# Split memory products: raw weights through four buffers, the second layer's normed memory earlier in a tile, and another order at the tail

## What is computed

```python
# first block, feed-forward: D = 1024, D_FF = 2816
ff = silu(h2 @ w_ffn_gate) * (h2 @ w_ffn_up)
x  = x + ff @ w_ffn_down
# second block, layer 0: conformer convolution, 31 taps
u = h @ w_pw1 + b_pw1;  a, gate = split(u);  u = a * sigmoid(gate)
u = depthwise_conv(u, 31 taps) + b_dw
u = silu(layernorm(u)) @ w_pw2 + b_pw2
# both layers l = 0, 1 of the second block: keys and values of the memory (256 rows)
mem_n = rmsnorm(mem, norm_memsrc_g[l])
k = mem_n @ mem_wk[l];  v = mem_n @ mem_wv[l]
```

## Time and profile before

| What | Value |
| --- | --- |
| Median of three runs | 2304.02 us (2301.10 to 2304.34) |
| The profiled execution's own time | 2304.21 us |
| Its span | 2302.0 us |
| PE busy | 2230.8 us (97%) |
| DVE, ACT, POOL busy | 1336.5, 979.6, 398.1 us |
| Mean granted PE clock, as a share of full | 0.988 |

### The profile page before, as it was taken

How to read it: one execution, slowest core, us unless ns; L and a number is a source line. 1 busy time by engine, 2 the same in 40 slices (tenths; PEclk the granted TensorE clock), 3 DMA queues, 4 the chain that set the end, 5 groups by cost and what they waited for, 6 DMA issues and landing times.

```text
span 2302.0 us, 31272 instructions
## 1 busy us (share of the span) xinstructions
PE 2230.8 (97%) x10680; PEld 1809.6 (79%) x10680; DVE 1336.5 (58%) x1904; ACT 979.6 (43%) x1486; POOL 398.1 (17%) x338
## 2 busy tenths in 40 slices
PE   8999999999999987889999999999999999999998
PEld 6787788877787776768888888887777888888887
DVE  5567756555554756876465445476565646454545
ACT  6775644433343555564333222245445333222222
POOL 2232002111010445644030000030000404000003
PEclk9999999999999988999999999999999999999999
DMA  4222223468686454461123333332221222333332
GB/s 146 64 65 70 68 83 100 137 170 254 170 236 191 130 192 142 155 206 55 56 83 92 96 98 100 91 93 79 65 65 56 83 65 74 102 98 93 100 92 91
DMA packets 413080, 253.36 MB, mean 110 GB/s; under 512 B 14832, under 2 KB 394224, under 8 KB 412976
## 3 DMA queue, kind: packets, MB, share of 16 engines
q1 hardware_dynamic: 412080, 249.68, 36.5%
q0 software_dynamic: 896, 2.33, 0.3%
HBM read 232.56 MB, written 18.87 MB: 109 GB/s over the span
## 4 chain that ended last, share of the span: by engine, by line
PE 73%; DMA 6%; DVE 5%; issue 4%; POOLq 4%; ACT 3%; SPq 2%; DVEq 1%; POOL 1%; ACTq 0%
PE bank L1944 20%; PE bank L1946 20%; PE bank L1945 20%; POOLq L667 4%; DMA m_raw<-in_w_ffn_up 4%; DMA m_raw<-in_w_ffn_down 2%; PE bank L1924 2%; DVE m_w_lo L1255 2%; PE bank L2417 1%; PE bank L2394 1%; PE bank L2097 1%; SPq L399 1%; PE bank L2523 1%; PE bank L2490 1%; ACT m_w_hi L692 1%
## 5 line engine op out<-in xcount | busy, mean ns | idle before, releaser
L692 ACT ACTIVATE m_w_hi<-m_raw 128x1024 fp32r<-128x1024 f32 x332 | 351.4, 1058 | 718.6 <-PE bank L1946 685.2
L1944 PE MATMUL bank<-m_h_hi,m_w_hi 128*128 128x512 f32 x1504 | 608.6, 405 | 12.5 <-DVE m_w_lo L1255 11.4
L1946 PE MATMUL bank<-m_h_hi,m_w_lo 128*128 128x512 f32 x1504 | 587.0, 390 | 0.0
L1945 PE MATMUL bank<-m_h_lo,m_w_hi 128*128 128x512 f32 x1504 | 586.5, 390 | 0.0
L1255 DVE TENSOR_TENSOR m_w_lo<-m_raw,m_w_hi 128x1024 fp32r<-128x1024 f32 x332 | 444.0, 1337 | 122.4 <-ACT m_w_hi L692 116.9
L1944 PEld LDWEIGHTS bank<-m_h_hi,m_w_hi 128*128 128x128 f32 x1504 | 282.9, 188 | 89.2 <-DVE m_w_lo L1255 19.1
L1946 PEld LDWEIGHTS bank<-m_h_hi,m_w_lo 128*128 128x128 f32 x1504 | 282.4, 188 | 60.3
L1945 PEld LDWEIGHTS bank<-m_h_lo,m_w_hi 128*128 128x128 f32 x1504 | 283.2, 188 | 54.9 <-issue 2.2
L1944 PE MATMUL bank<-m_f_hi,m_w_hi 128*128 128x512 f32 x688 | 269.2, 391 | 1.9 <-DVE m_w_lo L1255 1.7
L1946 PE MATMUL bank<-m_f_hi,m_w_lo 128*128 128x512 f32 x688 | 267.8, 389 | 0.0
L1945 PE MATMUL bank<-m_f_lo,m_w_hi 128*128 128x512 f32 x688 | 267.8, 389 | 0.0
(11 more groups left out here) (399 smaller groups left out, 3286.8 us busy)
## 6 DMA issues: line engine op xcount, KB each, us to landing
m_raw<-in_ff_w SPq DMA_DIRECT2D x256, 256.0 KB, 3.0
mem_low<-m_mem_raw_lo SPq DMA_DIRECT2D x32, 512.0 KB, 3.2
m_mem_w_low<-mem_low SPq DMA_DIRECT2D x32, 512.0 KB, 7.0
m_raw<-in_conv_pw_w SPq DMA_DIRECT2D x48, 256.0 KB, 3.1
m_raw<-in_w_in SPq DMA_DIRECT2D x47, 256.0 KB, 3.3
m_raw<-in_w_ffn_gate SPq DMA_DIRECT2D x44, 256.0 KB, 5.5
m_raw<-in_w_ffn_up SPq DMA_DIRECT2D x44, 256.0 KB, 5.3
m_raw<-in_w_ffn_down SPq DMA_DIRECT2D x40, 256.0 KB, 5.6
```

Source lines behind the costliest of these rows:

```text
L692: act.activation(WH[:, v % 2], RAW[:, v % 2], ACT.Copy).then_inc(s.w_hi, 1)
L1944: pe.matmul(o, high[:, r, k, :], hi, start=start, stop=False)
L1945: pe.matmul(o, high[:, r, k, :], lo, start=False, stop=False)
L1946: last = pe.matmul(o, low[:, r, k, :], hi, start=False, stop=stop)
```

## The change

Three parts. (1) In the FFN the raw memory weights go through four buffers at other addresses, are loaded ahead of unit n + 1 instead of n + 3, and wait for the store four memory units earlier. (2) In tiles 1 to 4 of the convolution `memory_high` stands ahead of ACT's first `mem_high` of the tile and `memory_low` ahead of the evacuation of unit A; in all tiles from 1 on, ACT forms products 6 to 8 ahead of the tile's further roundings, and 9 to 12 after them. (3) At the tail, ACT rounds memory units 25 and 26 ahead of tile 7's first products and evacuates unit 28 after the squares; PE forms the last mean ahead of memory unit 28.

```diff
-        SW = [at(f"mem_raw{i}", 144 + 4 * i, [P, D]) for i in range(3)]
-        SWL = [at(f"mem_raw_lo{i}", 144 + 4 * i, [P, D], F32R) for i in range(3)]
-        SWH = [at(f"mem_raw_hi{i}", 156 + 4 * i, [P, D], F32R) for i in range(2)]
+        SW = [at(f"mem_raw{i}", kb, [P, D]) for i, kb in enumerate((120, 124, 160, 194))]
+        SWL = [at(f"mem_raw_lo{i}", kb, [P, D], F32R) for i, kb in enumerate((120, 124, 160, 194))]
+        SWH = [at(f"mem_raw_hi{i}", kb, [P, D], F32R) for i, kb in enumerate((148, 152))]
...
+            def stored(i):
+                sp.wait_ge(sw_io[i % 4], 32 * (i // 4 + 1))
+
             def split_in(i):
-                if i >= 3:
-                    sp.wait_ge(sw_io[i % 3], 32 * (i // 3))
-                mem_raw(i, SW[i % 3], sw_io[i % 3])
+                if i >= 4:
+                    stored(i - 4)
+                mem_raw(i, SW[i % 4], sw_io[i % 4])
...
             for i, n in enumerate(MEM_SPLIT_AT):
                 split_at.setdefault(ffn + n + 5, []).append(lambda i=i: split_out(i))
             for i, n in enumerate(MEM_SPLIT_AT):
-                split_at.setdefault(ffn + n + 3, []).append(lambda i=i: split_in(i))
+                split_at.setdefault(ffn + n + 1, []).append(lambda i=i: split_in(i))
...
+                if 1 <= m <= 4:
+                    for k in range(2 * m - 2, 2 * m):
+                        memory_high(k, 1)
                 mem_high(first)
                 step(None)
+                if m > 0:
+                    products(m - 1, SUM_TAPS // 2, SUM_TAPS - 4)
                 for i in range(first + 1, min(last, first + 3)):
                     mem_high(i)
                 mem_out(first)
                 if m > 0:
-                    products(m - 1, SUM_TAPS // 2, SUM_TAPS)
-                if 1 <= m <= 4:
-                    for k in range(2 * m - 2, 2 * m):
-                        memory_high(k, 1)
+                    products(m - 1, SUM_TAPS - 4, SUM_TAPS)
                 step(None)
...
-            products(KD - 1, 0, 4, *last)
             mem_high(25)
             mem_high(26)
+            products(KD - 1, 0, 4, *last)
             mem_out(24)
...
             mem_out(27)
-            mem_out(28)
             for i in range(29, MEM_UNITS):
                 mem_high(i)
...
                 act.activation((LG, CA)[k % 2][:], CV[:, k, :], ACT.Square).then_inc(s.ln_sq, 1)
+            mem_out(28)
             norm(eps=EPSL, src=OB)
...
-                step(scaled(CA[:]), [chunk(0)])
-                if 1 <= m <= 4:
-                    for k in range(2 * m - 2, 2 * m):
-                        memory_low(k, 1)
+                def memory_lows():
+                    if 1 <= m <= 4:
+                        for k in range(2 * m - 2, 2 * m):
+                            memory_low(k, 1)
+
+                step(scaled(CA[:]), [chunk(0), memory_lows])
                 step(scaled(CG[:], None, s.cv_g), [chunk(1)])
...
-            for i in range(MEM_TAIL + 2, MEM_TAIL + 4):
-                mem_product(i)
+            mem_product(MEM_TAIL + 2)
             conv_mean(KD - 1).then_inc(s.ln_mean, 1)
+            mem_product(MEM_TAIL + 3)
```

More of the change, by code:

```diff
@@ L375, in build @@
         mw_in = [s.mw_in0, s.mw_in1, s.mw_in2, s.mw_in3, s.mw_in4]
-        sw_io = [s.sw_io0, s.sw_io1, s.sw_io2]
+        sw_io = [s.sw_io0, s.sw_io1, s.sw_io2, s.sw_io3]
         mem_low = nc.dram_tensor("mem_low", (MEM_UNITS, P, D), F32, kind="Internal").ap()
@@ L477, in mem_raw @@
                 sp.dma_start(dst[:].rearrange("p (a b) -> p a b", a=w.shape[1]), w).then_inc(done, 16)
+            def stored(i):
+                sp.wait_ge(sw_io[i % 4], 32 * (i // 4 + 1))
             def split_in(i):
-                if i >= 3:
-                    sp.wait_ge(sw_io[i % 3], 32 * (i // 3))
-                mem_raw(i, SW[i % 3], sw_io[i % 3])
+                if i >= 4:
+                    stored(i - 4)
+                mem_raw(i, SW[i % 4], sw_io[i % 4])
             def split_out(i):
                 sp.wait_ge(s.sw_lo, i + 1)
-                sp.dma_start(mem_low[i], SWL[i % 3][:].bitcast(F32)).then_inc(sw_io[i % 3], 16)
+                sp.dma_start(mem_low[i], SWL[i % 4][:].bitcast(F32)).then_inc(sw_io[i % 4], 16)
             ffn = U.n
@@ L492, in _ @@
             for i, n in enumerate(MEM_SPLIT_AT):
-                split_at.setdefault(ffn + n + 3, []).append(lambda i=i: split_in(i))
+                split_at.setdefault(ffn + n + 1, []).append(lambda i=i: split_in(i))
             def splits():
-                if U.n == ffn + MEM_SPLIT_AT[0] + 3:
+                if U.n == ffn + MEM_SPLIT_AT[0] + 1:
                     sp.wait_ge(s.unit_done, ffn)
@@ L517, in _ @@
                     assert not split_at
-                    for i in range(3):
-                        sp.wait_ge(sw_io[i], 32 * ((MEM_UNITS - 1 - i) // 3 + 1))
+                    for i in range(MEM_UNITS - 4, MEM_UNITS):
+                        stored(i)
                     for i in range(3):
@@ L957, in split_high @@
                 i = MEM_SPLIT_AT.index(U.n - 1 - ffn)
-                act.wait_ge(sw_io[i % 3], 32 * (i // 3) + 16)
+                act.wait_ge(sw_io[i % 4], 32 * (i // 4) + 16)
                 if i >= 2:
                     act.wait_ge(s.sw_lo, i - 1)
-                act.activation(SWH[i % 2][:], SW[i % 3][:], ACT.Copy).then_inc(s.sw_hi, 1)
+                act.activation(SWH[i % 2][:], SW[i % 4][:], ACT.Copy).then_inc(s.sw_hi, 1)
             def memory_high(k, layer):
@@ L1590, in split_low @@
                 dve.wait_ge(s.sw_hi, i + 1)
-                dve.tensor_tensor(SWL[i % 3][:], SW[i % 3][:], SWH[i % 2][:].bitcast(F32), ALU.subtract)\
+                dve.tensor_tensor(SWL[i % 4][:], SW[i % 4][:], SWH[i % 2][:].bitcast(F32), ALU.subtract)\
                     .then_inc(s.sw_lo, 1)
```

## The result

The changed kernel takes 2280.61 us (median of four runs, 2279.75 to 2281.56) against 2303.61 us of the kernel before on the same chip: a ratio of 0.9899, 95% interval 0.9886 to 0.9912, or 23 us less. The forecast was 2287, with a range of 2268 to 2302. The profiled run took 2279.9 us with a span of 2277.7, against a span of 2302.0 before: 24.3 less, and this is the number that the traces have to explain.

What follows compares the result with a forecast made beforehand. PE's unit matmuls were 60% of the chain, with PE waiting in the convolution and the FFN nearly full. Convolution -34, FFN +16 and tail +1 made -17 on a span of 2302.0, so 2287 us, range 2268 to 2302.

Steps and rivals of the forecast that it cites:

- The conv part: Convolution, seven tile periods: earlier normed memory and products shorten them from 181.3 us, -34 us (bounds -41 and -18).
- POOL's 19.1: Convolution, first tile period: 12 additions 1.46 us apart (17.5) plus 1.6 us between sums set the period at 19.1 us.
- The clock's share: Convolution tiles: PE granted clock 1.00 instead of 0.83 in tiles 1 to 4, counted inside the -34 us.
- The 2.8 us of waits that I gave back: Convolution: allowance of 0.4 us a tile for waits that couldn't be seen, taken off the -36.8 us gain.
- The wait for the store just issued: FFN units 21 to 25 and 45 to 49: SP stands still for a whole store ten times, +17.2 us in all.
- the period of 7.25: FFN each-unit stretches: SP needs 7.25 us per unit when each raw load waits for the preceding store.
- the store alone: FFN lower case: every store takes 3.2 us only and just the odd units count, sum +9 us instead of +16.
- The step that failed: FFN every-second-unit stretches: gaps stay, earlier raw load costed at 0; other bound, all 12.3 us of PE's wait go.
- the -1.4 of unit 53: FFN unit 53: one raw load less stands ahead of the unit's load, so PE's wait there goes, -1.4 us.
- The FFN is nearly full: FFN units 0 to 59: PE busy for 335.4 of 347.9 us, so only 12.5 us to be had.
- rival (b): FFN: raw weights ahead free ACT and PE's 12.3 us go too, -34 + 1 - 12, 2259 us; chance 0.06.
- The tail: Tile 7 to last mean: wait at memory unit 25 goes, one at unit 26 comes; +1 us, between -5 and +4.

Runs made afterwards that it cites:

- run 6: The whole change, raw loads still ahead of unit n + 1, but with five buffers instead of four: 2262.0 us, ratio 0.9824 to the kernel before.
- run 4: The whole change with its four buffers, but raw loads ahead of unit n + 2 instead of n + 1: 2251.93 us, ratio 0.9778 to the kernel before.

## Why the prediction was right, and where not

**The conv part** carried the sum. Forecast -34 with 147.3 us for the seven periods, measured 146.7 by itself. For the three periods of 21.3 (21.2 forecast) the working held: DVE has no gap there longer than 0.42 us. For the other four it didn't, and that the total came out is partly luck. The first was 20.7 where I had POOL's 19.1, and the last three were 20.7 where I had DVE's 20.6; in all four DVE waits 1.25 us for POOL's last addition, so POOL was the bound. The term that was mis-sized is POOL's: 12 additions 1.46 apart and 1.6 between two sums. I had used the lock between DVE and POOL for DVE's operations only, but it lengthens POOL's as well, by 1.6 us a sum. PE's term was too small too: the 18.8 us of the earlier trace rows came from a stretch with 2.0 us of idle time and 86 matmuls, and the same period now has 102 of them and a PE that is busy for all of its 20.7. The clock's share came as said, 0.90 to 1.00. That DVE's rest of the weights would be longer beside POOL than 1.23 was a choice, and it was right: 1.73 us at 883.13. The 2.8 us of waits that I gave back covered the first period's 1.6, but that was not found by reasoning.

**The wait for the store just issued** was the right mechanism, and the period of 7.25 was right (7.27 on average). The sum was +17.2 for both stretches. Against those of before they are 6.8 and 8.1 longer, 15.0, and the wait by itself (run 6) is 15.4. The difference is mostly at the start: raw load 21 went out at 523.83 where I had 528.4, because the store ahead of it was issued 3.9 us earlier than before and landed after 2.6 instead of 3.2. Of these 3.9 the program as a whole was 2.9 ahead by then (see below); the other 1.0 and the store's 0.6 shortened the first stretch's stall. The rule of the Trainium skill, page "DMA: Bandwidth & Descriptors", section "Queues, rings and completion order", that a DMA's semaphore lands only after every earlier write of its DMA engine, agrees with the stores: 2.6 us alone, 4.8 to 5.6 behind loads, and each time 1.2 to 1.3 after the last of these. A queue that works its transfers off one after the other would look the same, and no run here tells the two apart. It gave +16 and the store alone +9; the FFN came to +10.9, but not for the reason of the lower figure.

**The step that failed** is the one by which the FFN's other stretches were costed at 0. There the change had gained 2.5 us by unit 21. This and the 2.2 above are nearly the whole way from +16 to +10.9; the -1.4 of unit 53 came as said (-1.6 from unit 51 on). Why n + 1 is better than n + 3 ahead of unit 21 isn't settled: both put the raw load ahead of odd units, and in units 27 to 40 the same offset gained only 0.3. Five buffers have gained 3.0 by unit 21, n + 3 with four buffers 1.1, and the kernels with the FFN of before differ by 1.3 among themselves, so up to half of the 2.5 may be no effect of the change.

**"The FFN is nearly full"** was also too strong. I read 12.5 us to be had, from PE's busy time of 335.4 in 347.9. PE at its full pace takes 329.7: the busy time of a profile holds stretched matmuls at each stall, so the prize was 18.2 us. And rival (b), that PE's 12.3 us could go, got 0.06 with the argument that ACT's raw rounding isn't in the loop. True of this change, and true of why it gains nothing there. But the loop as I wrote it down (store, raw load, unit load, one behind the other ahead of the same unit) already held the remedy, moving the raw load by one unit, and run 4 found it by way of testing something else.

**The tail** was forecast at +1 and is worth nothing measurable (-0.3 by the traces, made of +2.4 in the seventh period and -2.7 behind it). Both waits appeared where they were said to.

So -34.6 + 10.9 - 0.3 - 0.3 ahead of the FFN = -24.3, where the forecast had -34 + 16 + 1. The best version that came of this, with all three parts, raw loads at n + 2 and unit 26 rounded later, takes 2249.8 us: 52 us or 2.3% less than the kernel before beside it, and by the spans 30 less than the change.

## What to carry to other kernels

When a queue of DMAs serves two purposes, look at which transfers are put ahead of the one that something waits for, and spread the background ones over the items that have slack: here one unit's offset was worth 28 us, an added buffer by itself nothing. A wait for a buffer should be for something at least one round old; with b buffers and an offset of d, write down which store each load waits for and how old it is in every stretch, since a pattern that is free in one stretch can stall in another. Busy time isn't the floor of a stretch: take the floor from the engine's pace in a part without a stall. When two engines lock each other out, lengthen the terms of both.

## What the runs showed of the hardware

- A 512 KB store to HBM landed 2.6 to 3.6 us after its issue with nothing ahead in the change's FFN. Issued behind 1 MB of loads in the rounds where SP waited for it, it took 4.8 to 5.6 us, 1.2 to 1.3 after the last of these loads.
- 256 KB halves of a unit landed after 3.7 and 4.1 us behind a store, after 6.2 behind a store and 512 KB of another load.
- Four units of run 4 moved 288 GB/s with the DMA share at 1.01 and PE without a gap.
- A DVE operation with two SBUF inputs and an addition of POOL took turns whichever began first: the second ended 1.1 to 1.2 us (the rest of a unit's weights, the addition) or some 0.6 us (the gate's product) after the first. In the profile the wait is part of the second's time: 1.23 became up to 2.03, 0.74 became 1.78, 1.3 became 2.08.
